# The opening of a two-block transformer kernel: value panel ahead of the tokens' copy of x, inverse row factors through DRAM

## The reference, cut to what matters

```
def rms_norm(x, g):
    y = xf * lax.rsqrt(jnp.mean(xf * xf, axis=-1, keepdims=True) + NORM_EPS)
    return (y * g.astype(jnp.float32)).astype(x.dtype)
...
h = rms_norm(x, pre_norm_g[i])
z = h @ w_in
q = z[..., :qk_w].reshape(B, S, RET_HEADS, RET_QK_DIM)
k = z[..., qk_w:2 * qk_w].reshape(B, S, RET_HEADS, RET_QK_DIM)
v = z[..., 2 * qk_w:2 * qk_w + RET_WIDTH].reshape(B, S, RET_HEADS, RET_V_DIM)
q = rope(q, pos)
k = rope(k, pos) * (RET_QK_DIM ** -0.5)
a = jnp.einsum('bhid,bhjd->bhij', qb, kb) * dmask
```

## Time and profile before

| | us |
|---|---|
| median of 3 runs | 2134.98 (2134.93 to 2135.9) |
| span of the profiled execution | 2133.8 |
| TensorE busy | 2114.8 (99%) |
| VectorE busy | 1469.4 (69%) |
| GpSimd busy | 1003.7 (47%) |
| ScalarE busy | 914.6 (43%) |

### The profile page before, as it was taken

How to read it: one execution, slowest core, us unless ns; L and a number is a source line. 1 busy time by engine, 2 the same in 40 slices (tenths; PEclk the granted TensorE clock), 3 DMA queues, 4 the chain that set the end, 5 groups by cost and what they waited for, 6 DMA issues and landing times.

```text
span 2133.8 us, 31557 instructions
## 1 busy us (share of the span) xinstructions
PE 2114.8 (99%) x11014; PEld 1794.3 (84%) x11014; DVE 1469.4 (69%) x2016; ACT 914.6 (43%) x1319; POOL 1003.7 (47%) x707
## 2 busy tenths in 40 slices
PE   9999999999999999999999999999999999999998
PEld 7888888777888888887788889988888888899887
DVE  7746556786777777778275787777655556877775
ACT  4423333554655555455445423333354445422333
POOL 4444544455433333435435655555433424655553
PEclk9999999999999999999999999999999999999998
DMA  6232222233222222232312223324222121223231
GB/s 225 87 108 78 87 81 98 90 109 109 85 88 84 79 79 79 79 129 79 119 65 106 90 97 104 112 98 138 79 80 80 60 80 60 99 99 106 100 105 62
DMA packets 38583, 202.18 MB, mean 95 GB/s; under 512 B 4427, under 2 KB 9675, under 8 KB 16236
## 3 DMA queue, kind: packets, MB, share of 16 engines
q1 hardware_dynamic: 34016, 193.56, 26.7%
q10 hardware_dynamic: 4492, 7.60, 1.1%
HBM read 195.90 MB, written 5.24 MB: 94 GB/s over the span
## 4 chain that ended last, share of the span: by engine, by line
PE 88%; DVE 5%; issue 2%; ACT 1%; DVEq 1%; DMA 1%; POOL 1%; SPq 0%; POOLq 0%; ACTq 0%
PE bank L488 14%; PE bank L489 13%; PE bank L494 13%; PE bank L475 10%; PE bank L476 10%; PE bank L477 10%; PE bank L1001 3%; PE bank L995 3%; PE bank L996 3%; PE bank L982 2%; PE bank L987 1%; DVE X L2210 1%; PE bank L1092 1%; DVE T L2207 1%; PE bank L785 1%
## 5 line engine op out<-in xcount | busy, mean ns | idle before, releaser
L406 POOL TENSOR_TENSOR WL<-RAW,WH 128x512 fp32r<-128x512 f32 x700 | 997.4, 1456 | 1102.5 <-ACT WH L1257 1102.5
L1257 ACT ACTIVATE WH<-RAW 128x2048 fp32r<-128x2048 f32 (+1 forms) x190 | 336.5, 1773 | 238.2 <-PE bank L494 121.8
L488 PE MATMUL bank<-HB,WH 128*128 128x512 f32 x776 | 308.1, 397 | 0.8 <-DVEq L2679 0.8
L489 PE MATMUL bank<-HB,WH 128*128 128x512 f32 x776 | 302.6, 390 | 0.0
L494 PE MATMUL bank<-HB,WL 128*128 128x512 f32 x776 | 194.0, 392 | 0.0
L488 PEld LDWEIGHTS bank<-HB,WH 128*128 128x128 f32 x776 | 145.8, 188 | 32.9 <-issue 1.4
L494 PEld LDWEIGHTS bank<-HB,WL 128*128 128x128 f32 x776 | 145.6, 188 | 32.4 <-issue 2.4
L489 PEld LDWEIGHTS bank<-HB,WH 128*128 128x128 f32 x776 | 145.8, 188 | 30.2 <-issue 1.0
L1257 ACT ACTIVATE HIDH<-T 128x512 fp32r<-128x512 f32 x64 | 40.0, 625 | 172.1 <-DVE T L2607 170.8
L1257 ACT ACTIVATE EH<-SUMS 128x1536 fp32r<-128x1536 f32 x24 | 35.7, 1489 | 175.7 <-DVEq L2567 175.7
L475 PE MATMUL bank<-HIDH,WH 128*128 128x512 f32 x256 | 99.7, 390 | 0.0
(11 more groups left out here) (495 smaller groups left out, 5237.3 us busy)
## 6 DMA issues: line engine op xcount, KB each, us to landing
RAW<-panels SPq DMA_DIRECT2D x174, 1024.0 KB, 4.8
xsave<-X ACTq DMA_DIRECT2D x4, 512.0 KB, 2.8
X<-xsave ACTq DMA_DIRECT2D x1, 2048.0 KB, 11.8
TAB<-scratch SPq DMA_DIRECT2D x16, 128.0 KB, 5.4
out<-ACC SPq DMA_DIRECT2D x8, 256.0 KB, 2.3
X<-xin SPq DMA_DIRECT2D x3, 512.0 KB, 9.0
T<-xtok SPq DMA_DIRECT2D x2, 512.0 KB, 11.8
U<-xtok SPq DMA_DIRECT2D x2, 512.0 KB, 13.6
```

Source lines behind the costliest of these rows:

```text
L406: gp.tensor_tensor(WL[:, s, cs], RAW[:, s, cs], WH[:, s, cs].bitcast(f32), ALU.subtract).then_inc(lo_ready, 1)
L488: nc.tensor.matmul(o, wh[:, columns[k - k0]], xh[:, k, :], start=first and k == k0, stop=False)
L489: nc.tensor.matmul(o, wh[:, columns[k - k0]], xl[:, k, :], start=False, stop=False)
L1257: return nc.scalar.activation(dst, src, ACT.Copy)
```

## The change

Five edits, all in the first head:

- SyncE issues the load of panel 2 ahead of the four loads of the tokens' copy.
- ScalarE splits panel 2 ahead of squaring the tokens.
- TensorE's four small products and ScalarE's copy of bank 0 to R go. In their place SyncE stores the four columns of RC to a small DRAM tensor (`factors`, 4x128) and loads it back to all 128 partitions of R. The load of panel 5 is issued between the store and the load.
- VectorE takes the reciprocal after the second reduction of the angle and not between the two; it waits for the load of R ahead of the first product with R. ScalarE waits for the reciprocal ahead of v.
- Counts of the semaphores `inverse_rows` and `rows_stored` are adjusted.

```
@@ the loads of SyncE
+            sp.wait_ge(lo_ready, PARTS)
+            load(2, 0)
             for tt in range(NT):
                 sp.dma_start(X_OF_TOKENS[tt], xtok[tt]).then_inc(S["tokens_loaded"], 16)
-            for m in range(2, 6):
+            for m in (3, 4):
                 sp.wait_ge(lo_ready, PARTS * (m - 1))
                 load(m, m % 2)
+
+            sp.wait_ge(S["inverse_ready"], 1)
+            sp.dma_start(factors.rearrange("t p -> p t"), INVERSE_OF_TOKENS,
+                         allow_slow_non_contiguous=True).then_inc(S["rows_stored"], 16)
+            sp.wait_ge(lo_ready, PARTS * 4)
+            load(5, 1)
+            sp.wait_ge(S["rows_stored"], 16)
+            sp.dma_start(R[:, :], factors.rearrange("t p -> (t p)").unsqueeze(0).to_broadcast([128, SEQ]))\
+              .then_inc(S["tokens_loaded"], 16)
@@ head, TensorE
                 end.then_inc(panel_used, 1)
-                if first:
-                    inverse_rows_of_tokens(0, 1)
@@ ScalarE
+            split_at(2)
             act.wait_ge(S["tokens_loaded"], 64)
             for tt in range(NT):
                 nc.scalar.activation(X_OF_TOKENS[tt], X_OF_TOKENS[tt], ACT.Square, accum_out=RC[:, 2 * tt:2 * tt + 1])
             act.drain()
             nc.scalar.activation(INVERSE_OF_TOKENS, INVERSE_OF_TOKENS, ACT.Sqrt, bias=EPSC[:, 0:1], scale=1.0 / D_MODEL)\
                 .then_inc(S["norm_root"], 1)
-            split_at(2)
-            act.wait_ge(S["inverse_rows"], 1)
-            hi(R[:, :], B[0][:, :]).then_inc(free[0], 1)
             split_at(3)
...
                 split_in(h, 8, 4)
+                if first:
+                    act.wait_ge(S["inverse_ready"], 1)
@@ angles, VectorE
                 less(t[0], t[0], 1.0 / turns, _parts(turns, 7, 6))
+                less(t[2], t[0], 1.0 / TWO_PI, _parts(TWO_PI, 8, 5))
                 between()
-                less(t[2], t[0], 1.0 / TWO_PI, _parts(TWO_PI, 8, 5))
@@ head, VectorE
-                        ve.wait_ge(free[0], 1)
+                        ve.wait_ge(S["tokens_loaded"], 80)
```

More of the change, by code:

```diff
@@ L144, in take, with program @@
         return self.i * self.per[b] + (v - self.first * self.per[b])
-def program(nc, panels, gains, xin, pin, pos, gn, decay, xtok, consts, every4, rel, onehot, wsT, bs, out, scratch, xsave):
+def program(nc, panels, gains, xin, pin, pos, gn, decay, xtok, consts, every4, rel, onehot, wsT, bs, out, scratch, xsave, factors):
     f32, f32r = mybir.dt.float32, mybir.dt.float32r
@@ L383, in _ @@
                 load_both(i)
-            sp.wait_ge(S["rows_stored"], 64)
+            sp.wait_ge(S["rows_stored"], 80)
             sp.wait_ge(panel_used, N_DIL - 2)
@@ L1363, in all_gained @@
                 root(name, D_MODEL, None, cols=True)
-                act.wait_ge(S["inverse_rows"], 3)
+                act.wait_ge(S["inverse_rows"], 2)
                 hi(RS[:, :], B[4][:, :]).then_inc(S["norm_hi"], 1)
@@ L1953, in _ @@
             root("final", D_MODEL, None, cols=True)
-            act.wait_ge(S["inverse_rows"], 5)
+            act.wait_ge(S["inverse_rows"], 4)
             hi(R[:, :], B[7][:, :]).then_inc(S["norm_hi"], 1)
@@ L2103, in head @@
                 twice_silu(1)
-                ve.wait_ge(S["rows_stored"], 64)
+                ve.wait_ge(S["rows_stored"], 80)
                 for vt in range(4):
@@ L2188, in per_layer_input @@
                     inverse = B[4]
-                    ve.wait_ge(S["inverse_rows"], 2)
+                    ve.wait_ge(S["inverse_rows"], 1)
                 for k in range(KD + 2):
@@ L2879, in _ @@
             inverse_columns("final")
-            ve.wait_ge(S["inverse_rows"], 4)
+            ve.wait_ge(S["inverse_rows"], 3)
             for k in range(KD - 2):
@@ L3062 @@
     xsave = nc.dram_tensor("xsave", (KD, 128, SEQ), mybir.dt.float32, kind="Internal").ap()
-    program(nc, out=out, scratch=scratch, xsave=xsave, **args)
+    factors = nc.dram_tensor("factors", (NT, 128), mybir.dt.float32, kind="Internal").ap()
+    program(nc, out=out, scratch=scratch, xsave=xsave, factors=factors, **args)
     r = run_bass_kernel_spmd(nc, [arrays], core_ids=[0])
```

## The result

| | before | after |
|---|---|---|
| median of 5 runs, us | 2134.93 (2134.68 to 2135.9) | 2145.82 (2143.14 to 2147.34) |
| ratio after to before | | 1.0047, 95% interval 1.0037 to 1.0058 |
| span of the profiled execution, us | 2133.8 | 2143.2 |

The changed kernel is **10.9 us slower**, 0.5%. The forecast was 2134.1 with a range up to 2137.0: it was wrong, and wrong on the side of a rival that had 4 in 100. The profiled execution of after took 2145.24, and that of before 2135.9, so a run's time is its span and about 2 us (2.0 and 2.1), not the 1 us that I had written.

The account below looks back on a forecast made before the run. TensorE, busy 2114.8 of 2133.8 us, was taken as the bound. 3.75 us saved at panel 2, less 2.75 waiting for KL and 0.1 restarting, gave 0.9 off 2134.98: 2134.1, range 2131.3 to 2137.0.

Parts of the forecast that it names:

- Step 1: Panel 2 loaded and split before the tokens: TensorE loses its 3.75 us detour and reaches the scores at 53.5.
- Step 2: Tokens' copy lands later, about 26.0; root at 31.9, panel 3 low about 40.6, covered by 8 us.
- Step 3: VectorE's rotation before the scores decides: clamp at 39.4, KL ends at 56.2, TensorE waits from 53.5.
- rival 1: VectorE's chain before the scores does not hold TensorE up: KL 0.7 to 2.7 us earlier, 2131.4 to 2133.4; chance 0.2.
- Step 4: R through DRAM: store takes 3.5 us, R lands at 45.4, or 45.7 behind panel 5, before VectorE needs it at 46.8.
- the bound of 9.6: Upper limit in us for the store of the factors: four times GN's load, each element costing a row of GN.
- Hidden, by about a microsecond: R's load lands by 45.7, ahead of VectorE's first product with R just before 46.8, so it costs nothing.
- rival 4: TensorE's clock falls in its 2.7 us wait before the scores, costing 1.7: 2135.8, up to 2136.6; chance 0.1.
- rival 3: Store at its upper bound, R landing past 51, plus TensorE's clock loss at the scores: 5.5 us slower, 2140.5; chance 0.04.
- 0.9 us faster: Whole-kernel gain: 3.75 us at panel 2 less 2.75 new wait for KL, less about 0.1 for restarting.

Follow-up runs that it names:

- m1: Kernel before plus five waited-for small stores: 512 neighbouring 4-byte elements 9.2 us, 256 such 8.15, 64-byte pitch 4.4, 512-byte pitch 1.8, 16-byte rows at most 2.3.
- e6: Changed kernel with the reciprocal back between the reductions, a store of 128 rows of 32 bytes, and R loaded ahead of panel 5: 2136.56 us, 1.0006.
- e7: Kernel before with panel 2 ahead of the tokens, the reciprocal later, and TensorE's small products moved into panel 3, without DRAM: 2136.26 us, 1.0002.
- e9: e7 with the loads of the constants and positions also ahead of panel 1: 2135.75 us, 1.0003 to the kernel before.
- e2: Changed kernel without the store, R loaded from a row of the decay table, output not the reference's: 2136.03 us, 1.0005 to the kernel before.
- e5: Changed kernel with the reciprocal back between the reductions and R's load ahead of panel 5's: 2139.47 us, 1.0021 to the kernel before.
- e11: Kernel before with the 4-byte store added ahead of panel 5, nothing in the opening waiting for it: 2135.54 us, 1.0002.
- after again: The changed kernel measured once more, unedited: 2144.6 us, 1.0047 to the kernel before.
- e1: Changed kernel with only the reciprocal put back between the two reductions, so the store is issued earlier: 2140.1 us, 1.0021 to the kernel before.
- e4: Changed kernel storing all of RC as 128 rows of 32 bytes, ScalarE picking the factors out after loading: 2140.69 us, 1.0025 to the kernel before.

## Why the prediction was wrong

**Step 1 (panel 2 ahead) was right.** Split at 21.15 to 23.1 (21.0 to 22.9 forecast), low by 31.2 (31.1), no wait of TensorE at 31.77, its own work done at 53.7 (53.5).

**Step 2 (tokens behind) was right.** ScalarE's and GpSimd's timelines of after:

```profile
25.75 1.06 ACT L1406 ACTIVATE T<-T 128x1024 f32<-128x1024 f32 x1 [2.68 <-DMA U<-xtok]
...
31.37 0.30 ACT L1408 ACTIVATE RC<-RC,EPSC 128x4 f32<-128x4 f32 x1
```

```profile
18.55 12.67 POOL L417 TENSOR_TENSOR WL<-RAW,WH 128x512 fp32r<-128x512 f32 x8 [3.92 <-ACT WH L1266]
34.11 6.49 POOL L417 TENSOR_TENSOR WL<-RAW,WH 128x512 fp32r<-128x512 f32 x4 [2.89 <-ACT WH L1266]
```

The squares start at 25.75 (26.0), the root ends at 31.67 (31.9), panel 3 is low at 40.60 (40.6).

**Step 3 (VectorE next in line) was right.** The first six steps end at 31.76 (31.6), the clamp starts at 39.83 (39.4), T at 42.57 (42.4). Taking VectorE's step as 1.69 beside GpSimd and 0.75 without held within 0.5 us over twenty microseconds; "VectorE is not in the way" (rival 1) fell with it.

**Step 4 (R through DRAM) failed, in both of its terms.** "I take 3.5" for the store: it took 11.18, above even the bound of 9.6, and 10.4 to 12.2 in the openings of the other kernels (9.2 alone in m1). "By RS, R lands 2.5 later", 2.8 behind the panel: R took 5.25, and 4.9 to 5.2 in the other runs of that store. "Hidden, by about a microsecond" became a wait of 9.79. RS's 2.5 was taken where little else was in flight, while R was in flight with panel 5 and RS; in e6, where it went alone, 512 KB took 3.3. That this is why R took twice as long is likely, not shown. Together the store and R came to 16.4 us where I had 6.3. With the store issued 0.36 later, that is 10.5 us; less 1.1 of slack gives 9.4, which is 65.69 less the forecast 56.25. Of the two terms the store was off by 7.68 and R's load by 2.45.

How I came to 3.5: every small transfer that I looked at, GN and RS, reads DRAM. None writes it. The trace of before has only large stores to scratch, for whose landing nothing in the opening waits (their reader comes past 68), so no row there could price a write's acknowledgement. I took "four times GN" for a bound from above, but it was one only if the cost went by the number of pieces; m1 shows that it goes by their being neighbours.

**The clock** (rival 4's mechanism, inside rival 3) came as an addition: 2.4 us behind the wait of 12 against the 1.7 that I had taken from the tail. Whether the 2.7 us wait of my forecast would have kept the clock stays open: with 1.9 and 2.4 us of wait (e6, e7, e9, e2) it stayed at 1.00, behind 3.2 (e5) it fell.

**The sum** in the traces: the scores begin 8.46 us later and 2.38 are lost behind them, 10.84 together, near the 10.9 between the medians. The 8.46 are 9.44 lost by step 4 less the 0.98 that steps 1 to 3 were to gain; the 0.98 is the forecast's and was seen in no run by itself, but steps 1 to 3 came out within 0.5 us. The mechanism was rival 3's, with R's landing at 56.2, far past the 51 from which I had let it decide; its price was half of the true one (5.5 us, 2140.5), with 9.6 for the store, 2.5 for R and 1.7 for the clock. I gave it 4 in 100 because I held the upper bound to be improbable; with no row for the operation on which the whole change turned, it deserved a third, and the range should have gone past the bound.

**"0.9 us faster" without step 4** is neither shown nor refuted. Every variant without the slow store (e2, e6, e7, e9) lies at 1.0002 to 1.0006, with intervals of about 0.1% to each side: a gain of 0.9 us (0.04%) can hardly be seen there; only e6's interval, from 0.9997, ends just short of it. In the profiles all of them wait 1.9 to 2.4 us for KL, with scores between 57.16 and 59.53 where before's stand at 57.23. These positions can't be set against before's as they are, since its opening ran at full clock and theirs did not (0.52 to 0.76 from 12 to 18 us). The two with like openings are e9 and e11, which has the order of before (first line e9, second e11, columns as in the windows above):

```profile
12.00:18.00 6.00, 6.00 (x15) 4.70 (x16) 4.66 (x7) 3.44 (x6) 2.53 (x2) 0.52 1.03 395
12.00:18.00 6.00, 6.00 (x14) 3.84 (x13) 4.13 (x5) 4.61 (x7) 2.55 (x2) 0.50 1.03 410
```

Their scores begin at 59.53 and 59.13: in e9 what is won at panel 2 is given back at the scores, where KL came late by the late place of the small products. No version measurably beat the kernel before.

## What to carry to other kernels

A round through DRAM on the critical path has to be priced by a row that writes DRAM and waits for it; if the trace has none, that is the term to bound generously and to measure first. If small values must go that way, write them as rows of 16 bytes or more, or spread them out, never as 4-byte neighbours: the same 2 KB took 9.2 or 1.8 us (what it costs to read them back spread out was not measured). And before panel traffic is put first, look for what is next in line, for here 3.75 us won in one place came back as waits in another.

## What the runs showed of the hardware that was not expected

- **A store of 512 neighbouring 4-byte elements** to DRAM is acknowledged 9.2 to 12.2 us after its issue, though its packets are out in under 3; panel loads issued around it land in 9.4 to 12.9 us where 4.8 to 5.2 was usual (e11, after), and GN's 2 KB in 12.9 where it took 2.4 (after). The time does not suffer as long as nobody waits for them (e11).
- **The opening's clock differs between executions of one kernel.** The profiled run of before and the first of after show 1.00 from 12 to 18 us; that of after again shows 0.52, e9 0.52, e11 0.50, e5, e7 and e2 0.72, and the scores shift with it. I found nothing in the kernels that orders this. A slower opening is not always a slower run: after again had VectorE's first T at 40.01 and not 42.57, and with 2141.66 it was the fastest of its five.
- **So does the tail's.** The 16 small products that took 3.75 us took 2.02 in after, and 2.02 to 3.39 elsewhere. Before's profiled run had lost 1.7 us there, which is most of why the spans differ by 9.4 and the medians by 10.9.
- **Waits of TensorE and what followed them** at the scores: behind 1.9 and 2.4 us the clock stood at 1.00; behind 3.2 (e5), 4.9 (e1), 5.8 (after again), 6.4 (e4) and 12.0 (after) a stretch followed that the windows show at 0.50 to 0.53 where it is lowest. In e5 the first five products behind the wait still took 0.39 to 0.50, and the fall came only then (0.60 from 60 to 61 us, 0.50 from 61 to 63). From the first product of the scores to the row of eight these five took 8.91 to 9.82 us, where 7.44 to 7.58 is usual. The Trainium skill, TensorE: Matmul & The Clock Gate, Part 1, has the clock fall behind idle time; the traces agree for the waits of 3.2 us and more.
